# Attention scores in pairs: one head from each half of TensorE's rows, in two PSUM banks

## The reference, cut to what matters

```python
def gqa_attend(q, k, v):
    s = jnp.einsum('bqkgd,bskd->bkgqs', q, k).astype(jnp.float32) * (ATT_HD ** -0.5)
    p = jax.nn.softmax(s, axis=-1).astype(v.dtype)
    return jnp.einsum('bkgqs,bskd->bqkgd', p, v)
...
    k_all = jnp.concatenate([ck, xk], axis=1)
    v_all = jnp.concatenate([cv, xv], axis=1)
...
    o = lax.map(lambda qb: gqa_attend(qb, k_all, v_all), q_blk)
```

## Time and profile before

| | |
|---|---|
| median of 3 runs | 1538.28 us (1536.97 to 1543.53) |
| the profiled execution | 1539.22 us |
| its span, first to last instruction | 1537.9 us |
| mean granted TensorE clock | 0.935 of full |
| TensorE busy | 1362.5 us, 89% |
| VectorE, ScalarE, GpSimd busy | 854.1, 617.5, 265.0 us |
| instructions | 18885 |

### The profile page before, as it was taken

How to read it: one execution, slowest core, us unless ns; L and a number is a source line. 1 busy time by engine, 2 the same in 40 slices (tenths; PEclk the granted TensorE clock), 3 DMA queues, 4 the chain that set the end, 5 groups by cost and what they waited for, 6 DMA issues and landing times.

```text
span 1537.9 us, 18885 instructions
## 1 busy us (share of the span) xinstructions
PE 1362.5 (89%) x7490; PEld 1061.6 (69%) x7490; DVE 854.1 (56%) x1469; ACT 617.5 (40%) x1000; POOL 265.0 (17%) x224
## 2 busy tenths in 40 slices
PE   4998886998773999867789999999999987999998
PEld 3876665876662877645577677777778866777686
DVE  2766554776557123379776344233476887544544
ACT  3444423444424252511032365432355345545453
POOL 0200101200115010334210011021133124120012
PEclk8999887999885999988699999999999999999999
DMA  8532347432443212111012112122263312332342
GB/s 303 184 123 83 124 166 288 164 108 83 153 163 112 91 69 69 42 41 42 28 55 69 55 41 82 56 83 92 73 202 131 110 42 96 118 111 89 108 151 96
DMA packets 48040, 165.19 MB, mean 107 GB/s; under 512 B 5734, under 2 KB 6950, under 8 KB 47696
## 3 DMA queue, kind: packets, MB, share of 16 engines
q1 hardware_dynamic: 47952, 163.98, 31.5%
HBM read 162.91 MB, written 1.05 MB: 107 GB/s over the span
## 4 chain that ended last, share of the span: by engine, by line
PE 67%; DVE 14%; issue 7%; ACT 4%; POOL 4%; DMA 3%; SPq 0%; POOLq 0%; ACTq 0%; DVEq 0%
PE bank L1189 15%; PE bank L1191 14%; PE bank L1190 14%; DVE conv_val L2236 4%; PE bank L1104 4%; PE bank L1474 3%; DVE w_lo L1922 2%; PE bank L1498 2%; PE bank L1207 2%; DMA w_raw<-in_w 2%; PE bank L1209 2%; PE bank L1208 2%; PE bank L1123 1%; PE bank L1185 1%; ACT w_hi L1540 1%
## 5 line engine op out<-in xcount | busy, mean ns | idle before, releaser
L1189 PE MATMUL bank<-w_hi,x_hi 128*128 128x512 f32 (+4 forms) x1120 | 470.0, 420 | 1.2 <-DVE x_lo L1932 1.2
L1922 DVE TENSOR_TENSOR w_lo<-w_raw,w_hi 128x1024 fp32r<-128x1024 f32 (+3 forms) x256 | 314.1, 1232 | 261.4 <-ACT w_hi L1540 260.9
L1191 PE MATMUL bank<-w_hi,x_lo 128*128 128x512 f32 (+4 forms) x1120 | 433.6, 387 | 0.0
L1190 PE MATMUL bank<-w_lo,x_hi 128*128 128x512 f32 (+4 forms) x1120 | 432.9, 387 | 0.0
L1540 ACT ACTIVATE w_hi<-w_raw 128x1024 fp32r<-128x1024 f32 (+3 forms) x256 | 263.1, 1029 | 341.0 <-PE bank L1191 154.5
L1189 PEld LDWEIGHTS bank<-w_hi,x_hi 128*128 128x128 f32 x1120 | 216.1, 193 | 54.4 <-issue 18.2
L1191 PEld LDWEIGHTS bank<-w_hi,x_lo 128*128 128x128 f32 x1120 | 214.3, 191 | 43.9
L1190 PEld LDWEIGHTS bank<-w_lo,x_hi 128*128 128x128 f32 x1120 | 215.6, 193 | 34.4
L2236 DVE SCALAR_TENSOR_TENSOR conv_val<-conv_u,par,conv_val 128x512 f32<-128x512 f32 (+1 forms) x240 | 146.4, 667 | 0.0
L1207 PE MATMUL bank<-x_hi,w_hi 128*128 128x512 f32 (+1 forms) x192 | 70.7, 368 | 0.0
L2561 POOL TENSOR_TENSOR merged<-merged,sigma 128x512 f32<-128x512 f32 x24 | 33.4, 1411 | 216.6 <-DVE sigma L2278 216.6
(11 more groups left out here) (340 smaller groups left out, 1846.5 us busy)
## 6 DMA issues: line engine op xcount, KB each, us to landing
w_raw<-in_w SPq DMA_DIRECT2D x168, 512.0 KB, 3.5
w_raw<-in_wm SPq DMA_DIRECT2D x48, 512.0 KB, 4.4
w_raw<-in_wo SPq DMA_DIRECT2D x40, 512.0 KB, 3.6
w_raw<-in_wy_gla SPq DMA_DIRECT2D x8, 512.0 KB, 3.5
w_raw<-in_wy_conv SPq DMA_DIRECT2D x8, 512.0 KB, 3.6
w_raw<-in_wy_att SPq DMA_DIRECT2D x8, 512.0 KB, 3.6
w_raw<-in_w SPq DMA_DIRECT2D x8, 460.0 KB, 6.0
par<-in_small SPq DMA_DIRECT2D x2, 1218.0 KB, 9.4
```

The lines of the kernel that those rows point to most:

```text
L1189: mm(out, xh[:, q, col], hi[:, kk, 0:w], start=q == 0 and kind != "in2", stop=False)
L1190: mm(out, xh[:, q, col], lo[:, kk, 0:w], start=False, stop=False)
L1191: ins = mm(out, xl[:, q, col], hi[:, kk, 0:w], start=False, stop=last and kk == KP - 1)
L1922: v.tensor_tensor(lo, raw, hi.bitcast(F32), ALU.subtract).then_inc(sem["cut_lo"], 1)
```

## The change

`attention` now yields its stages by pairs of calls, (0, 1), (2, 3) and so on. The two score calls are in one group of steps, which stays together. Softmax, flips and values come as two groups a tick. There are half as many ticks. The new `places` says which of the eight places in `PAIRED` a call takes: for an x tile the call's own number, so that calls 2i and 2i+1 are one head on the lower and one on the upper rows; for a context tile call 0 takes places 0 and 2, call 1 places 1 and 3, and calls 2 and 3 the same four further on, so that each call still has two heads of the same rows in one bank and the next call is on the other rows. The maxima, sums and reciprocals are now kept in the order of `PAIRED`, written and read with a step of two for context tiles, and `att_out2` reads them so.

```diff
--- before.py
+++ after.py
@@ -522,16 +522,22 @@
     for j in range(4):
         yield [("aq_flip", l, j), ("aq_act" if j % 2 == 0 else "aq_dve", l, j)]
     for qt in tiles_of(l):
-        scores = lambda j: iter([[("a_s", l, qt, j)]])
-        top = lambda j: iter([[("a_max", l, qt, j), ("a_exp", l, qt, j), ("a_inv", l, qt, j)]])
-        turn = lambda j: iter([[("a_flip", l, qt, j), ("a_t_act" if j % 2 else "a_t_dve", l, qt, j)]])
-        values = lambda j: iter([[("a_v", l, qt, j)]])
-        yield from pipeline(range(maps_of(qt)), [scores, top, turn, values], [0, 1, 2, 3])
+        pair = lambda i: (2 * i, 2 * i + 1)
+        scores = lambda i: iter([[("a_s", l, qt, j) for j in pair(i)]])
+        top = lambda i: iter([[("a_max", l, qt, j), ("a_exp", l, qt, j), ("a_inv", l, qt, j)] for j in pair(i)])
+        turn = lambda i: iter([[("a_flip", l, qt, j), ("a_t_act" if j % 2 else "a_t_dve", l, qt, j)] for j in pair(i)])
+        values = lambda i: iter([[("a_v", l, qt, j)] for j in pair(i)])
+        yield from pipeline(range(maps_of(qt) // 2), [scores, top, turn, values], [0, 1, 2, 3])
         yield [("att_out2", l, qt)]
 
 
 def maps_of(qt):
     return 8 if qt in X_TILES else 4
+
+
+def places(qt, j):
+
+    return [j] if qt in X_TILES else [4 * (j // 2) + j % 2, 4 * (j // 2) + j % 2 + 2]
 
 
 def pieces_of_stream():
@@ -1469,7 +1475,7 @@
         pe.wait_ge("aq_act", l, 2)
         pe.wait_ge(*(before or ()))
         for g in range(n_maps):
-            h = j * n_maps + g
+            h = PAIRED[places(qt, j)[g]]
             rows = slice(h // 4 * HD, (h // 4 + 1) * HD)
             ins = mm(k.bank[i][:, g * keys:(g + 1) * keys], b.aq_t[rows, h % 4, qt * P:(qt + 1) * P],
                      b.ak_t[rows, k0:k0 + keys], start=True, stop=True)
@@ -1492,8 +1498,8 @@
             pe.wait_ge("ev2", l, KKV, 3)
             pe.wait_ge(*(before or ()))
         for g in range(n_maps):
-            h = j * n_maps + g
-            kh, at = h // 4, (h % 4) * 2 + h // 4
+            at = places(qt, j)[g]
+            kh = PAIRED[at] // 4
             for c, t in enumerate(key_tiles):
                 ins = mm(k.bank[i][:, at * HD:(at + 1) * HD], turned[:, (g * nb + c) * P:(g * nb + c + 1) * P],
                          b.kkv[:, t, QK2 + P + kh * HD:QK2 + P + (kh + 1) * HD], start=c == 0, stop=c == nb - 1)
@@ -1860,7 +1866,7 @@
         act.wait_ge("a_max", l, qt, j)
         act.wait_ge(*(before or ()))
         for g in range(n_maps):
-            h = j * n_maps + g
+            h = places(qt, j)[g]
             ins = do(b.aprob[:, p, g * keys:(g + 1) * keys], ps[:, g * keys:(g + 1) * keys], ACT.Exp,
                      bias=stat[:, h:h + 1], accum_out=stat[:, AH + h:AH + h + 1])
         ins.then_inc(sem["a_exp"], 1)
@@ -2402,22 +2408,20 @@
         v.tensor_scalar(b.aq_t[:, j, 0:n], ps[:, 0:n], HD ** -0.5, None, ALU.mult).then_inc(sem["aq_dve"], 1)
 
     def a_max(l, qt, j):
-        n_maps = 8 // maps_of(qt)
-        h = j * n_maps
+        n_maps, at = 8 // maps_of(qt), places(qt, j)
         ps = k.bank[slot("aux", "a_s", l, qt, j)[0]]
         i, before = slot("a_stat", l, qt)
         if j == 0:
             dve.wait_ge(*(before or ()))
         dve.wait_ge("a_s", l, qt, j)
-        v.tensor_reduce(b.astat[:, i, h:h + n_maps], ps[:, :].rearrange("p (a b) -> p a b", a=n_maps), AXX, ALU.max,
+        v.tensor_reduce(b.astat[:, i, at[0]:at[-1] + 1:2], ps[:, :].rearrange("p (a b) -> p a b", a=n_maps), AXX, ALU.max,
                         negate=True).then_inc(sem["a_max"], 1)
 
     def a_inv(l, qt, j):
-        n_maps = 8 // maps_of(qt)
-        h = j * n_maps
+        at = places(qt, j)
         stat = b.astat[:, slot("a_stat", l, qt)[0], :]
         dve.wait_ge("a_exp", l, qt, j)
-        v.reciprocal(stat[:, 2 * AH + h:2 * AH + h + n_maps], stat[:, AH + h:AH + h + n_maps]).then_inc(sem["a_inv"], 1)
+        v.reciprocal(stat[:, 2 * AH + at[0]:2 * AH + at[-1] + 1:2], stat[:, AH + at[0]:AH + at[-1] + 1:2]).then_inc(sem["a_inv"], 1)
 
     def a_t_dve(l, qt, j):
         ps = k.bank[slot("aux", "a_flip", l, qt, j)[0]]
@@ -2434,7 +2438,7 @@
         dve.wait_ge("a_inv", l, qt, maps_of(qt) - 1)
         dve.wait_ge("aq_flip", l, 3)
         v.tensor_tensor(pairs(b.aq[:, qt, :]), pairs(ps[:, :]),
-                        inv.rearrange("p (b a) -> p a b", b=2).unsqueeze(3).to_broadcast([P, AH // 2, 2, HD]),
+                        inv.rearrange("p (a b) -> p a b", b=2).unsqueeze(3).to_broadcast([P, AH // 2, 2, HD]),
                         ALU.mult).then_inc(sem["att_out2"], 1)
 
     def gate_diag(l, s, c, i):
```

## The result

| | before | after |
|---|---|---|
| median | 1538.99 us (6 runs, 1535.70 to 1543.53) | 1550.09 us (6 runs, 1546.03 to 1554.32) |
| profiled execution | 1539.22 | 1549.11 |
| span, granted clock | 1537.9, 0.935 | 1547.8, 0.928 |

The ratio is 1.0073, with a 95% interval of 1.0049 to 1.0097: the change makes the kernel 11 us **slower**. I had forecast 11 us less; the outcome is that of rival 4.

The account below looks back on a forecast made before the run. TensorE was taken as the bound in the attention. -24.4 for pairs, +1.0, +3.45, +6.05 and +3.3 for waits, -2.1 for waits gone and +1.7 for the clock gave -11.0 us: forecast 1527.4 us, range 1518 to 1543.5.

Parts of the forecast that it names:

- rival 4: Three auxiliary banks make flips, copies and scores a chain; waits and four clock falls: +7.8 us, 1546.1; chance 0.10.
- The gain: 20 adjacent score pairs, two calls side by side on opposite rows, each saving 1.22 us: -24.4 us.
- B1: Layer 0, second x tile, conv_mean in bank 4: flips and scores without projections between, second score waits for an exponential; +3.45 us.
- Rival 2: Passes keep program order, so only A2 and B1 overlap; a pair saves 0.82 us; sum -3.0, 1535.3; chance 0.13.
- A: Layer 0, first x tile, behind conv taps: first score waits 1.4 us, second flip 1.75; net +1.0 us.
- B2: Layer 0, second x tile, conv_var in bank 6: a 10.3 us chain behind the last conv_n; +6.05 us.
- E: Granted clock: B2 may bring one fall, nothing to 3.4 us, middle taken: +1.7 us; A keeps its earlier fall.
- C: Layer 1: at three places a second flip follows the first in its bank, plus two short waits; +3.3 us.
- D: Three waits of 0.69 us of a values call for ScalarE's copy are gone; -2.1 us.
- F: Counted at nothing: context tiles, VectorE's strided columns, weights' cuts, SP's and POOL's queues, three table loads fewer on ScalarE.

Follow-up runs that it names:

- same_rows: The changed kernel with its order, banks and waits, but each pair takes heads of the same 64 rows; 1556.05 us, 1.0124 of the kernel before.
- pairs_layer1: The kernel before with pairs only in layer 1, single calls in all other tiles; 1540.25 us, 1.0020 of the kernel before.

## Why the prediction was wrong

**The gain, -24.4.** The mechanism and both its parts are right (1.06 us for the pair, 0.85 and 0.39 measured). Its size was off, since I multiplied by 20: six pairs were parted. I had seen for B1 that the second score waits for an exponential, put the delay into the wait, and still counted the pair's saving. same_rows puts the side-by-side part at 11.2 us in the attention (14 pairs x 0.85 are 11.9); with 20 x 0.39 that makes 19 us, an estimate.

**Rival 2** is out, for passes of scores: A1 A2 B1 B2 fit in 1.06 us only as two passes' time, and three would need 3 x 0.427 + 0.2 = 1.48. A context pair shows it for whole matmuls, two of each call on its own rows: the next projection starts at 949.81, 1.07 us behind

```profile
948.74 1.14 PE L1480 MATMUL bank<-att_k_t,att_q_t 64*128 64x256 f32 x8
```

which is four rounds of a pass of 256 columns and not six or more; in same_rows the eight passes take 1.92. So the third matmul in program order streams with the first, ahead of the second. The strict order that the Trainium skill states in "TensorE: Matmul & The Clock Gate", Part 3, The mechanism, does not hold between the two halves of the rows here; the earlier trace rows had said so.

**A** came as worked out for the first score (1.40 us of wait, predicted 1.4). The second flip waited 2.90 and not 1.75, and 0.70 more for an exponential. The stretch's -4.7 against my -3.9 looks right by luck: 3.0 of it is the clock's fall, which I took as fixed and which is chance, so the four pairs brought 1.7 us.

**B1 and B2 with E** are the step that failed by its size: +9.5 of waits and +1.7 of clock, against four pairs' -4.9, were to give +6.3 in that tile; it took +10.8, and +15.5 with pairs there alone. The place, the lines and the kind of chain were right (a wait of 2.9 us for the last conv_n where I had 2.2). What I mis-sized is that I priced the clock as an addend, nothing or 3.4 us, when the chain runs inside the low clock: 14.6 us instead of 10.3, and the clock stayed at 0.50 for 13.7 us, to 931.9, 3 us past the chain's end at 928.91.

**C, layer 1.** +3.3 was predicted, on top of eight pairs; the stretch came out at +0.9 instead of -7.9, the largest miss with the second tile's. The flips are as said but for one more (four waits, 3.3 us); missing in my sum are the second scores, held by an exponential of the pair before: 2.6 us of waits, three parted pairs that lose 0.85 each, and a fall of the clock behind the worst of them:

```profile
1453.99 1.12 PE L1480 MATMUL bank<-att_k_t,att_q_t 64*128 64x512 f32 x2
1456.98 1.56 PE L1480 MATMUL bank<-att_k_t,att_q_t 64*128 64x512 f32 x2 [1.86 <-ACT att_p L1870]
```

ScalarE had the copy, a weight's cut and a table load ahead of that exponential, and VectorE the same weight's low cut ahead of the maximum that it needs, which ended last (0.59 us of wait):

```profile
1452.71 0.60 ACT L1879 ACTIVATE att_pt<-bank 128x512 f32<-128x512 f32 x1 [2.61 <-PE bank L1110]
1453.21 1.05 ACT L1546 ACTIVATE w_hi<-w_raw 128x1024 fp32r<-128x1024 f32 x1
1454.28 1.28 ACT L1870 ACT_TABLE_LOAD   x1
1454.29 1.22 DVE L1928 TENSOR_TENSOR w_lo<-w_raw,w_hi 128x1024 fp32r<-128x1024 f32 x1 [2.33 <-ACT w_hi L1546]
1455.43 0.68 DVE L2417 TENSOR_REDUCE att_stat<-bank 128x1 f32<-128x512 f32 x1
1456.15 0.69 ACT L1870 ACTIVATE att_p<-bank,att_stat 128x512 f32<-128x512 f32 x1 [0.59 <-DVE att_stat L2417]
```

and from 1458.0 to 1460.6 the granted clock was 0.50, a fall that I had given to layer 0 alone.

**D** came, the values call waits for ScalarE no more. **F** was wrong for the context tiles: I counted three table loads fewer and no loss, but what counts is where two stand close together, and there it cost 1.56 us.

**The sum.** Counted from a kernel before whose clock does not fall at 805 (3.0 us), the attention lost 4.0 + 3.0 = 7.0 us where I had forecast 11.0 less, a miss of 18.0. The pairs gained 19 and not 24.4, which is 5.4 of it. TensorE's waits grew by 20.1 - 4.8 = 15.3 where I had 13.8 - 2.1 = 11.7, which is 3.6. The low clock, 13.7 us from 918.2 and 3.4 us from 1457.5, cost up to half of these 17.1 us, 8.6, where I had 1.7: 6.9, the largest part. The last 2.1 are not told apart. Waits and clock together took 26.0, twice the 13.4 that I had; with D's 2.1 put back, as in rival 4, that is 28.1, over its point of 26.5. But rival 4 had four falls of 3.4, and the attention had two, of which one was long.

Of the 11 us in the medians 4 to 7 are so accounted for, the more the fewer executions of the kernel before have that fall. The others are not: the profiled execution has 5.9 us outside the attention, other kernels with the same order there from -0.4 to +3.8. Of the 5.9, 2.8 lie ahead of 788.31, where no order has changed, so they are chance. The other two parts, 1.6 us each, are at 1109 and at 1519, each with the clock at 0.50 for 3.4 us where before had 1.00; no run here separates chance from effect in them.

## What to carry to other kernels

Where a saving is bought by pairing steps, price each member's own wait: a pair whose second member waits for a bank is two single steps, and the saving goes with the overlap. Part the members of each other stage (here flips and softmax) with independent work, and pace a side queue that a resource has held up, or its backlog becomes a chain with nothing beside it. And where a wait may pull the clock down ahead of a chain, cost the chain's own steps at the low clock too, as here 14.6 us for 10.3.

## What the runs showed of the hardware that I had not expected

The same wait before the first score sometimes pulled the clock down and sometimes not. Before, 2.15 us of pause were followed by 0.50 until 811.8; in pairs_layer1, whose order is the same there, the timeline and the windows have

```profile
803.84 1.12 PE L1480 MATMUL bank<-att_k_t,att_q_t 64*128 64x512 f32 x2 [2.09 <-DVE att_q_t L2408]
...
800.00:804.00 4.00, 1.91 (x11) 1.30 (x10) 4.00 (x7) 2.34 (x2) 0.00 (x0) 1.00 0.20 83
804.00:810.00 6.00, 6.00 (x21) 3.48 (x22) 5.16 (x9) 0.78 (x2) 0.00 (x0) 1.00 0.32 87
```

the full clock after 2.09. Here that was worth 3.0 us of a kernel's time by chance, a quarter of this change's effect.

The same is true of the pauses from which I had argued in E that a pause need not cost the clock (1505 to 1510 in the earlier trace rows, TensorE busy for 2.01 of 5 us, clock 1.00 there and behind it). The changed kernel has the same steps with the same pauses, and there they were followed by a fall:

```profile
1513.50:1518.50 5.00, 2.04 (x14) 1.57 (x15) 3.56 (x9) 2.28 (x4) 2.40 (x2) 1.00 0.31 105
1519.00:1522.40 3.40, 3.40 (x15) 3.13 (x14) 0.81 (x4) 1.62 (x3) 0.00 (x0) 0.50 0.02 5
```
